# Feed-forward products of a split-precision transformer kernel: two of three matmuls merged into one of 512 columns, halves summed on VectorE

## What is computed

```python
def swiglu(h, w_gate, w_up, w_down):            # w_gate, w_up: 1024 x 2816; w_down: 2816 x 1024
    return (jax.nn.silu(h @ w_gate) * (h @ w_up)) @ w_down
...
mod = jax.nn.silu(c) @ w_ada[l] + b_ada[l]      # 1024 x 6144, needed by the second block
...
xs = jax.vmap(lambda hb, ib: hb[ib])(h, idx)    # 16 experts, 32 tokens each
hid = jax.nn.silu(jnp.einsum('becd,edf->becf', xs, w_gate)) * jnp.einsum('becd,edf->becf', xs, w_up)
out = jnp.einsum('becf,efd->becd', hid, w_down) * gates[..., None].astype(h.dtype)
```

## Time and profile before

| what | value |
|---|---|
| median of 3 runs | 2270.21 us (2270.06 to 2271.98) |
| profiled execution: time, span | 2270.32 us, 2268.5 us |
| busy share of the span: TensorE, VectorE, ScalarE, GpSimd | 79%, 36%, 23%, 4% |
| HBM read | 736.88 MB, 325 GB/s over the span |
| first feed-forward block, second one | about 265 to 456 us, 688 to 876 us |
| expert stage | from about 1003 us to the end |

### The profile page before, as it was taken

One profiled execution on the slowest core, in us unless ns is written; L12 is line 12 of the kernel. 1 busy time (PEld: TensorE's weight loads), 2 busy tenths in 40 slices (PEclk: granted clock), 3 DMA queues, 4 the chain that ended last, 5 costly groups with the idle time before them and its releaser, 6 DMA issues.

```text
span 2268.5 us, 28734 instructions
## 1 busy us (share of the span) xinstructions
PE 1801.5 (79%) x12614; PEld 1155.9 (51%) x12614; DVE 815.1 (36%) x1237; ACT 529.3 (23%) x797; POOL 88.0 (4%) x136
## 2 busy tenths in 40 slices
PE   7999999999999999998656666665665666666676
PEld 7898999999889998863111221111111112111121
DVE  5855677767567776851100100101010010010101
ACT  5745533356444334630000000000000000000000
POOL 1200000012100000000000000000000000000000
PEclk9999999999999999999878778877887787787788
DMA  8455666754546775499999999999999999999997
GB/s 256 136 166 178 195 223 232 238 165 158 187 155 200 252 247 177 160 405 429 428 429 430 428 429 430 429 429 429 429 429 429 430 429 429 429 429 428 430 430 305
DMA packets 171933, 739.80 MB, mean 326 GB/s; under 512 B 6768, under 2 KB 133232, under 8 KB 146976
## 3 DMA queue, kind: packets, MB, share of 16 engines
q1 hardware_dynamic: 169456, 731.27, 81.1%
q0 software_dynamic: 2352, 6.69, 0.9%
HBM read 736.88 MB, written 1.05 MB: 325 GB/s over the span
## 4 chain that ended last, share of the span: by engine, by line
DMA 49%; PE 42%; DVE 5%; ACT 3%; issue 1%; POOL 0%; SPq 0%; DVEq 0%; POOLq 0%; ACTq 0%
PE PS L367 41%; DMA WB<-in_w_up 24%; DMA WB<-in_w_down 24%; DVE WL L1698 1%; ACT WH L1154 1%; DVE S L1693 1%; DVE X L1693 1%; DMA W<-in_w_gate 0%; PE PS L466 0%; POOL T L2538 0%; DMA W<-in_w_in 0%; DVE S L1690 0%; ACT HTh L1215 0%; DVE CN L1690 0%; PE PS L595 0%
## 5 line engine op out<-in xcount | busy, mean ns | idle before, releaser
L367 PE MATMUL PS<-WB,XS 128*32 128x352 f32 x3360 | 397.2, 634 | 238.6 <-DMA WB<-in_w_up 161.2
L367 PEld LDWEIGHTS PS<-WB,XS 128*32 128x32 f32 x3360 | 125.6, 140 | 507.8 <-DMA WB<-in_w_up 216.4
L1698 DVE TENSOR_TENSOR WL<-W,WH 128x2048 fp32r<-128x2048 f32 x138 | 317.0, 2297 | 135.1 <-ACT WH L1154 135.0
L1693 DVE SCALAR_TENSOR_TENSOR S<-S,PS 128x352 f32<-128x352 f32 (+1 forms) x110 | 63.4, 588 | 752.9 <-PE PS L367 420.9
L367 PE MATMUL PS<-WB,S 128*32 128x512 f32 (+1 forms) x1216 | 237.4, 740 | 116.8 <-DMA WB<-in_w_down 94.0
L367 PE MATMUL PS<-HTh,WH 128*128 128x256 f32 x1064 | 307.8, 289 | 8.9 <-DVE HTl L1693 6.4
L1154 ACT ACTIVATE WH<-W 128x2048 fp32r<-128x2048 f32 x141 | 269.5, 1912 | 184.0 <-PE PS L367 179.0
L367 PE MATMUL PS<-HTl,WH 128*128 128x256 f32 x1064 | 302.0, 284 | 0.0
L367 PE MATMUL PS<-HTh,WL 128*128 128x256 f32 x1064 | 301.9, 284 | 0.0
L367 PEld LDWEIGHTS PS<-HTh,WH 128*128 128x128 f32 x1064 | 204.9, 193 | 13.5 <-DVE WL L1698 6.3
L367 PEld LDWEIGHTS PS<-HTl,WH 128*128 128x128 f32 x1064 | 205.1, 193 | 0.9
(11 more groups left out here) (281 smaller groups left out, 2154.4 us busy)
## 6 DMA issues: line engine op xcount, KB each, us to landing
WB<-in_w_up SPq DMA_DIRECT2D x63, 2816.0 KB, 35.9
WB<-in_w_gate SPq DMA_DIRECT2D x47, 2816.0 KB, 35.9
WB<-in_w_down SPq DMA_DIRECT2D x47, 2816.0 KB, 36.0
CN<-in_w_gate SPq DMA_DIRECT2D x16, 2816.0 KB, 36.5
CN<-in_w_down SPq DMA_DIRECT2D x16, 2816.0 KB, 36.1
W<-in_w_in SPq DMA_DIRECT2D x31, 1024.0 KB, 5.4
S<-in_w_ada SPq DMA_DIRECT2D x24, 1024.0 KB, 5.4
W<-in_w_gate SPq DMA_DIRECT2D x22, 1024.0 KB, 7.9
```

Source lines behind the costliest of these rows:

```text
L367: return e.matmul(o, l, r, start=start, stop=stop, skip_group_check=True)
L1693: return e.scalar_tensor_tensor(out=o, in0=a, scalar=s, in1=b, op0=o1, op1=o2)
L1698: e.tensor_tensor(M.WL[i][:, :], M.SLOT[m % NW], M.WH[i][:, :].bitcast(F32), ALU.subtract).then_inc(*up("low", m))
```

## The change

1. `HTh` and `HTl` become one tensor `HT2` with two planes. In gate and up units the two products with the high weights become one matmul of 512 columns (`proj_halves`), into a whole bank; the product with the low weights adds onto columns 0 to 255. Each half j of the features has a bank of its own: gate in banks 0 and 1, up in 2 and 3. So the wanted product is the sum of the two halves of a bank.
2. ScalarE copies the upper halves of two banks to SBUF (`FG`, `FU`), VectorE adds the lower halves to it in two adds of 128x256. Tanh and the gating products read `FG` and `FU`.
3. The sum of a modulation job now stands behind the up unit on TensorE, always in bank 0, and its bias add on VectorE behind the adds of the up halves.
4. In the expert stage, the gather of the last group comes after the products of chunks 0 and 1.

Memory and TensorE's program:

```diff
+        M.HT2 = sb("HT", [128, 2, 8, 256], F32R, first)
+        M.HT = [M.HT2[:, i] for i in range(2)]
...
+    M.FG, M.FU = view(1024, 2, 256), view(1536, 2, 256)
...
+    def given(name, i):
+        i, k = C.banks.give(name, i)
+        if k > 1:
+            e.wait_ge(C.sig.sem(f"bank{i}"), k - 1)
+        return PS[:, 4 + i, :]
...
+    def proj_halves(name, l, n, to, b, norm=None):
+
+        m, u = unit(name, l, "cols", n)
+        for j in range(2):
+            ps = given((*to, j), b + j)
+            for k in range(8):
+                if norm and j == 0:
+                    e.wait_ge(*at("lo", norm, k))
+                w = part(u, slice(None), k, slice(128 * j, 128 * j + 128))
+                mm(two(ps), w[0], M.HT2[:, :, k, :], k == 0, False)
+                ins = mm(ps[:, 0:256], w[1], HT[0][:, k, :], False, k == 7)
+            if j:
+                ins.then_inc(*up("unit", m))
+            beside.step()
+        for j in range(2):
+            same(("full", *to, j), ("unit", m))
...
-        ps, acc, ones = take(("ada", n)), products(i, M), M.CST[:, C_ONES:C_ONES + 128]
+        ps, acc, ones = given(("ada", n), 0), products(i, M), M.CST[:, C_ONES:C_ONES + 128]
...
         for n in range(11):
-            proj_t("w_gate", l, n, HT, ("g", l, n), norm=("ffn", l) if n == 0 else None)
+            proj_halves("w_gate", l, n, ("g", l, n), 0, ("ffn", l) if n == 0 else None)
+            proj_halves("w_up", l, n, ("u", l, n), 2)
             ada_sum(12 * l + n)
-            proj_t("w_up", l, n, HT, ("u", l, n))
...
             if ex == m == 0:
-                for i in range(4):
+                for i in range(3):
                     gather_first(i)
...
+                if ex == m == 0 and k == 1:
+                    gather_first(3)
```

In ScalarE's `ffn`:

```diff
+        def halves(o, what, l, n, b):
+            full(what, l, n, 1)
+            if n:
+                e.wait_ge(*at("f_prod", l, n - 1))
+            e.activation(o, PS[:, 4 + b:6 + b, 256:512], ACT.Copy).then_inc(*up("f_half", what, l, n))
+
         for n in range(11):
             A, i = M.A[n % 2], n % 4
             unit()
             unit()
-            g = two(full("g", l, n))
-            if n >= 2:
-                e.wait_ge(*at("hid", l, n - 2))
-            e.activation(flat(A), flat(g), ACT.Tanh, scale=0.5).then_inc(*up("f_tanh", l, n))
+            halves(M.FG, "g", l, n, 0)
             if n > 1:
                 unit()
             else:
                 early()
-            e.wait_ge(*free("u", l, n))
+            if n >= 2:
+                e.wait_ge(*at("hid", l, n - 2))
+            for j in range(2):
+                e.wait_ge(*free("g", l, n, j))
+            e.activation(flat(A), flat(M.FG), ACT.Tanh, scale=0.5).then_inc(*up("f_tanh", l, n))
+            halves(M.FU, "u", l, n, 2)
+            e.wait_ge(*at("f_prod", l, n))
```

In VectorE's `ffn`, one step:

```diff
             unit()
             next(job)
-            ada_sum(12 * l + n)
             unit()
             next(job)
-            g, u = flat(two(full("g", l, n))), flat(two(full("u", l, n)))
-            e.wait_ge(*at("f_tanh", l, n))
-            stt(flat(A), flat(A), 1.0, g, ALU.add, ALU.mult).then_inc(*freed("g", l, n))
+
+            def halves(o, what):
+                e.wait_ge(*at("f_half", what, l, n))
+                for j in range(2):
+                    e.tensor_tensor(o[:, j, :], full(what, l, n, j)[:, 0:256], o[:, j, :], ALU.add).then_inc(*freed(what, l, n, j))
+
+            halves(M.FG, "g")
             next(job)
             if n > 1:
                 unit()
             next(job)
             if n < 2:
                 early()
-            e.wait_ge(*free("g", l, n))
-            stt(flat(A), flat(A), 0.5, u, ALU.mult, ALU.mult).then_inc(*freed("u", l, n))
+            e.wait_ge(*at("f_tanh", l, n))
+            stt(flat(A), flat(A), 1.0, flat(M.FG), ALU.add, ALU.mult).then_inc(*step())
+            halves(M.FU, "u")
+            ada_sum(12 * l + n)
+            own()
+            for j in range(2):
+                e.wait_ge(*free("u", l, n, j))
+            stt(flat(A), flat(A), 0.5, flat(M.FU), ALU.mult, ALU.mult).then_inc(*up("f_prod", l, n))
             e.wait_ge(*at("f_hi", l, n))
```

More of the change, by code:

```diff
@@ L256, in memory @@
         M.MEM = [sb(n, [128, 8, 256], F32R, first) for n in ("MEMh", "MEMl")]
-        M.HT = [sb(n, [128, 8, 256], F32R, first) for n in ("HTh", "HTl")]
+        M.HT2 = sb("HT", [128, 2, 8, 256], F32R, first)
+        M.HT = [M.HT2[:, i] for i in range(2)]
         M.W = sb("W", [128, 2048 * NW], F32, first)
```

## The result

The changed kernel takes **2309.6 us** (median of 4 runs, 2308.39 to 2309.74); the kernel before, run beside it, 2271.1 (2270.06 to 2273.58). The ratio is 1.017, with a 95% interval of 1.0158 to 1.0182: slower. The forecast was 2297.4 with a range of 2286 to 2308; direction and mechanism hold, the size is short by a third, and the range is missed by 1.6 us. The profiled execution has a span of 2307.9 us against 2268.5, so 39.4 us are to be accounted for, where 27.1 were forecast.

The account below looks back on a forecast made before the run. TensorE bounds the engine stage up to about 1000 us, then the expert weight stream. Layer 0 +18.2, layer 1 +9.2 and gather -0.3 give +27.1 us on 2270.32: 2297.4 us, range 2286 to 2308.

Parts of the forecast that it names:

- Per step: Both feed-forward blocks: TensorE's new waits less its savings, summed step by step to +18.2 us in layer 0, +9.2 in layer 1.
- G(0): First gate unit of layer 0's block: waits until the last fill is copied out of bank 0, +1.7 us after its saving.
- layer 0, three strided steps: Layer 0's last three steps, strided products, no modulation sum: period set by the chain, +1.25 us each, 3.75 in all.
- part 1: Gate and up units on TensorE: 512-column matmuls at 0.228 make each unit 5.57 us instead of 5.76, saving 8.5 us.
- rival (a): Gate and up units: 512 columns cost as two matmuls, 0.240, so no gain; about +7.8 us, 2305; chance 0.14.
- The steady steps: Layer 0's five contiguous steps: next gate unit waits for bank 0 until 6.8 us after the up unit; 17.95 against 17.39 us.
- The first steps: Layer 0's first two steps, no down unit to hide behind: bank 0 free 5.9 us after the up unit, +5.1 each, 10.3.
- The gather: Expert 0: moving one gather releases the first weight buffer 1.4 us earlier; with a full DMA queue 0.3 us gain taken.
- Does the delay reach the end?: Expert loads are issued behind the feed-forward blocks, nothing in the stream can start earlier, so the delay is added whole.
- rival (d): Whole kernel: the weight stream soaks up the delay, or nothing that matters moves; 2270 us, chance 0.04.
- Rival (b): Bank 0 and the tail after the up unit: VectorE's extra work hides, TensorE saves 8.5 us; 2261.8, chance 0.08.
- Rival (c): Feed-forward blocks: only the first steps stall, the tail is hidden in steady state; +8 us, 2278, chance 0.07.

Follow-up runs that it names:

- run 2: Changed kernel plus 11 unused identity matmuls on TensorE behind the modulation sum in layer 0's first two steps; 2305.4 us.
- run 3: Changed kernel with the bank rotation moved on by two before layer 0's feed-forward block, so the last fill avoids bank 0; 2306.02 us.
- run 10: Changed kernel with modulation sum ahead of the up unit in bank 3, rotation moved by two, next up unit's weights rounded before the step's last two operations; 2268.0 us.
- run 4: Changed kernel with the modulation sum ahead of the up unit in bank 3 and its VectorE addition back at its old place; 2293.32 us.
- run 5: Changed kernel with one more unused pair of 256-column adds a step on VectorE, between gating product and up half's adds; 2327.23 us.
- run 7: Changed kernel with the next up unit's weights rounded ahead of the step's last two operations, nothing else moved; 2301.3 us.
- run 8: As run 10, but with VectorE's last modulation pair of each step also moved behind the product's low part; 2312.14 us.

## Why the prediction was right or wrong

**The step that failed** is in "Per step", where the waits at the head of the blocks are priced: "5.9 - 0.4 - 0.38 = +5.1, twice: 10.3" and "+1.7" for G(0). The waits came as forecast (5.47 and 5.24 us, and one of 3.0). What was left out is that the unit behind a wait was counted at 5.57 us, full clock. G(1) took 8.2, from 285.65 to the first start of U(1) at 293.82. The terms, forecast and measured (lengths of units in the last column run from their first start to their last):

| term | forecast | measured | of it |
|---|---|---|---|
| layer 0, G(0) and U(0) | +1.7 - 0.4 = +1.3 | +2.8 | wait 3.0; G(0) takes 7.1, clock 0.79 |
| layer 0, next two steps | +10.3 | +16.1 | clock 5.3, the rest 10.8 (run 2) |
| layer 0, five contiguous steps | +2.8 | +3.5 | +0.66 a step, +0.85 the first |
| layer 0, three strided steps | +3.75 | +4.3 | |
| layer 0, behind U(10) | 0 | +0.3 | |
| layer 1, up to U(4) | +3.65 - 0.2 = +3.45 | +5.1 | U(3) takes 7.2 behind a wait of 2.4, clock 0.70 |
| layer 1, six steps | +4.8 | +6.1 | +0.94 to +1.16 a step |
| layer 1, behind U(10) | +1.0 | +1.3 | |
| second block | 0 | +1.3 | in kernels without the change too |
| gather | -0.3 | -0.9 | -1.3 as the mean of all traces |

The measured terms add up to 39.9; the 0.2 us by which layer 0's block begins sooner, 0.1 between the blocks and rounding make the span's 39.4 of it.

The clock is shown by run 2 for 5.3 us. At G(0) run 3 shows it: without the wait that unit takes 5.8 us, 1.3 less. In layer 1 it was read in one window and in the unit's length (7.2 us in place of 5.5) and not tested by a run of its own. Together that is some 8 of the 12.3 us that the forecast lacks, 1.3 more lie in the second block, and the rest is spread over the steps. In the steady ones it is small: G(n+1) starts 6.9 us behind the end of U(n), where the count had 6.8, and the two units take 11.17 where it had 11.14. What the 0.1 to 0.3 us a step in the strided steps and in layer 1 consist of wasn't taken apart.

Two of the prediction's sums don't come out of its own rows. For G(0) it has a start at 267.0 in place of 264.68, 2.3 us later, and takes off 1.0 on the way to +1.3, where the pair's saving is 0.4. And its upper bound of 2306 is more than its terms give (2297.4 and 4.2 for the adds); neither bound has a term for the clock.

**512 columns.** Right in kind: a saving is there, and the starts lie in the bounds of part 1 (0.225 to 0.240; measured 0.23 to 0.24 from start to start). Where TensorE alone sets the steps (run 10), 0.30 of the forecast 0.38 us a step arrived in layer 0 and 0.19 in layer 1, so rival (a), no gain, is wrong for layer 0 and halfway right for layer 1. The prediction took 5.75 for both units from the gate unit's row; the up unit's in the same rows is 5.83. The Trainium skill's sustained 131 ns for 512 columns (page "TensorE: Matmul & The Clock Gate", section "Back-to-back issue gap") is contradicted by the starts here, of float32r operands, as by those of before.

**The steady steps.** The size was right (17.95 forecast, 18.07 measured), the reason only half: the sum went through bank 0, and run 4 shows that without bank 0 the steps stay at 18.1. Both chains run through VectorE's tail, so the price of the adds is right for either, as run 5 shows. I noted both and priced one.

**The first steps.** Right in place, count and length of the waits (5.47 and 5.24 us), wrong in their price; run 4 gives 15.2 us back when the sum leaves bank 0.

**The gather.** I took 0.3 in bounds of 0 to 1.4, "near the row of a full queue". The load behind the first buffer is issued 1.3 us sooner, as the 1.4 of the row said, and the end comes 1.3 us sooner in the mean, so nearly all of it arrives although the DMA rows stand at 1.01. Why a full queue lets it through is not shown.

**Does the delay reach the end?** Right: the blocks' 39.0 us are in the span whole, and rival (d) has nothing for it. Rival (b), faster, needed both counts of bank 0 to be wrong; run 10 shows what it would have taken: the sum elsewhere, the fill elsewhere and the next up unit's weights ahead. Rival (c) is refuted by 18.07 in the steady steps.

## What to carry to other kernels

Price a new wait of TensorE of several microseconds twice: its length, and the unit behind it at half the clock until rows show the clock back; here two waits of 10.7 us together made two steps 16.1 us longer. Before crediting or charging a steady step, write down every chain that closes on itself within it, not the longest one: of two chains within 0.1 us of each other, cutting one left the contiguous steps at 18.1 (run 4), cutting the other left them at 18.1 to 18.2 (run 7), and cutting both gave 17.11 (run 10). And of a moved instruction ask which buffer its end releases and what is queued behind that transfer: 0.9 us of VectorE's work a step, moved behind 4 us of other work, cost 44 us through SyncE's queue (run 8 against run 10).

## What the runs showed of the hardware

- Behind a standstill of 5.5 us TensorE ran at its lower level for the first 9 of a unit's 16 pairs of matmuls (0.64 us a pair, then 0.35), though it was busy throughout. Filling the standstill with matmuls that nobody needs brought the clock to 1.00 and the program 4.2 us. A wait of 2.4 us also had it (0.70 in 4 us); that behind 5.25 us was shorter in one run (0.76 over 10 us) than in another (0.63 over 9 us). Behind 1.8 us one trace shows a unit at full length (5.6 us, changed kernel, layer 1) and another the lower level (7.1 us at 0.76, run 10, the same unit); behind waits of 1.6 us it took 5.6.
- The same instructions with the same busy share (4.6 of 6 us) ran at a clock of 1.00 in two traces and at 0.72 and 0.78 in two others, of the kernels before and after and two near relatives of the first. A difference of 1 to 2 us between two traces is not yet the change's.
- A matmul of 512 columns whose moving operand is two runs of 256 starts 0.23 to 0.24 us before the next, like one of 512 in a row (0.228).
